# Two-block kernel: output and down projections as seven block products instead of eight

## The chip, the cores and the metric

The program runs on one core of a Trainium2 chip, in float32 throughout. The metric is the device time of one execution in microseconds (us), the median of several runs. Engines are named PE (matmuls), VectorE (DVE in rows), ScalarE (ACT), GpSimd (POOL) and SyncE (SP, which issues the weight loads).

## The reference, cut to what matters

The model has a first block (four mixers and a routed mixture of experts) and, behind it, two layers of a second kind of block, which are where the change lies. For 528 rows (16 meta rows and 4 tiles of 128 tokens) each layer computes, with `alpha = 4 ** 0.25`:

```python
m = concat(retention, pooling, attention)      # rows x 1024
h = layer_norm(alpha * h + m @ w_out)           # output projection, 1024 x 1024
u = silu(h @ w_ffn1) * (h @ w_ffn3)             # rows x 2816
h = layer_norm(alpha * h + u @ w_ffn2)          # down projection, 2816 x 1024
```

## The kernel before

Only the two layers matter here. Each layer `l` is worked in two runs, named by `x`: run A holds tiles 1 and 2 (and the meta rows, tile 0, in layer 0), run B tiles 3 and 4. `TILES`, `WHOLE` and `SPAN` say which rows that is. PE's program for the layers is `layers()`: `project` (input projection), `mix` (output projection), `turn_rows` (transposes of normalised rows, copied out by ScalarE), `feed_up` (gate and up projections, one pair for each of 22 blocks `f` of 128 features) and `feed_down`. The feed is done in two chunks, `FF_CHUNKS`: c = 0 has 12 blocks, c = 1 has 10. The order around the joints is: `mix(0,A)`, the last four feature items of `project(0,B)`; `feed(0,A)`, `mix(0,B)`, `project(1,A)`; `feed(0,B)`, `mix(1,A)`, `project(1,B)`; for (1,A) both chunks of `feed_up` and the first `feed_down`, then `mix(1,B)`, then `feed_down(1,A,1)`, then `turn_rows("mid",1,B)` and `feed(1,B)`.

**Projections as items.** An output projection of a run is four items (two tiles by two halves of 512 output columns), each a chain of 8 matmuls 128x512 over k into one PSUM bank (L1579). A down projection is four items of 12 or 10 matmuls (L1610). With run A in layer 0 comes an item for the 16 meta rows (L1570, L1613). One `pe.matmul` in float32 is two passes in the trace, so 8 matmuls are 16 rows there. VectorE adds each bank to the residual `h2` (L3129, L3191), and normalises a tile when its second half is there (`norm_rows`, L2746 to L2764; `norm_centered` and `norm_scaled` at the end of a feed). In both, ScalarE gives the root of the variance between two steps (`rows_root`, L1869); where in ScalarE's order this stands is written out by hand in its `layers()`, for example `roots(3)` ahead of `project(1,A)`, which begins with the copies of `turn_rows("start",1,A)`.

**Banks.** All items share the ring `main` of three banks. An item waits until the bank of the item three before it is drained.

**Weights.** Pieces of 2 MB go in program order through a ring of four slots (`LAYER_SLOTS`), loaded by SyncE (L1785). Piece n is loaded when piece n-4 is done with, which is marked by `piece_free[at] = main.done()`. `weights(l, n)` makes PE wait for the piece's landing. An output projection has two pieces, one for each half of the columns; a down chunk has three. Piece order at two joints, with the slots: the three of `feed_down(0,A,1)` in slots 2, 3 and 0, then the two of `mix(0,B)` in 1 and 2; the two of `mix(1,B)` in 2 and 3, then the three of `feed_down(1,A,1)` in 0, 1 and 2.

**Attention.** `attend(l, x)` is a generator of steps (`Plan`), run on every engine with the same numbering and taken one by one with `each(steps)` between items: before every block of `feed_up` and before every item of `feed_down`. Steps from `fox_at` on (17 in plan B, 14 in plan A) are softmax attention: PE writes scores (L1485), VectorE adds the bias and takes the maximum (L3061 to L3075), ScalarE exponentiates, VectorE scales (L3084), and the next step's transposes on PE wait for that (`fox_weights_ready`).

**GpSimd** only issues the loads of the norms' parameters in the layers (L1831), each behind the event that frees the buffer `ln_par2`.

## Time and profile before

| | |
|---|---|
| median of 3 runs | 3264.47 us (3263.72 to 3269.08) |
| span of the profiled execution | 3252.7 us |
| PE busy | 3120.2 us, 96% of the span |
| VectorE, ScalarE, GpSimd busy | 975.8, 540.8, 47.2 us |
| layers | about 1735 us to the end of the span |

The profiled execution is one of its own; the page gives its span, not its time between host and end. The span is 11.8 us under the median of the runs: start and end of the program lie around it. PE's busy time says how long at least one pass was in flight; the time of one pass is its group's busy time by its count.

### The profile page before, as it was taken

The numbers are of one execution on the slowest core, as the hardware profiler recorded it, in microseconds if no ns is written. First come the engines' busy times: TensorE is split into PE (matmuls) and PEld (weight loads), VectorE is DVE, ScalarE is ACT, GpSimd is POOL, SyncE is SP. The second block draws the span as 40 slices with busy tenths as digits, with TensorE's granted clock in tenths as the row PEclk, the third lists the DMA queues.
The fourth block names the chain that finished last, engine by engine and source line by source line (L and its number), as shares of the span: only waits on it lengthen the run. The fifth ranks groups of instructions, "written<-read, shape, count | busy, mean of one in ns | idle before, by whom it ended". The sixth has DMA issues, their size and how long they took to land.

```text
span 3252.7 us, 52666 instructions
## 1 busy us (share of the span) xinstructions
PE 3120.2 (96%) x22631; PEld 1747.5 (54%) x22631; DVE 975.8 (30%) x2146; ACT 540.8 (17%) x1129; POOL 47.2 (1%) x58
## 2 busy tenths in 40 slices
PE   9878989999999999999999999999999999999999
PEld 3355545333343333333345668574785758675866
DVE  1633455232223223222363431223023122132101
ACT  1332311111111111111122220130102100040000
POOL 0000002000000000000010000000000000000000
PEclk9888979999999999999989999999999999999999
DMA  9800115999999999999863333234333243243532
GB/s 400 354 1 27 53 53 224 386 410 403 408 397 406 400 406 407 407 407 404 351 251 119 125 130 117 111 143 176 135 126 142 105 194 133 100 176 116 195 145 100
DMA packets 97466, 743.70 MB, mean 229 GB/s; under 512 B 11128, under 2 KB 38336, under 8 KB 57552
## 3 DMA queue, kind: packets, MB, share of 16 engines
q1 hardware_dynamic: 58768, 687.49, 53.6%
q10 hardware_dynamic: 32624, 30.52, 2.9%
q0 software_dynamic: 5968, 24.14, 1.9%
q8 instruction: 83, 1.36, 0.2%
q14 instruction: 23, 0.19, 0.0%
HBM read 674.98 MB, written 67.13 MB: 228 GB/s over the span
## 4 chain that ended last, share of the span: by engine, by line
PE 55%; DMA 28%; DVE 3%; ACT 2%; issue 1%; ACTq 1%; POOL 0%; DVEq 0%
DMA arena<-x_sorted 27%; PE psum L1593 19%; PE psum L1610 9%; PE psum L1540 5%; PE psum L1579 3%; PE psum L1551 3%; PE psum L1244 1%; PE psum L802 1%; ACTq L587 1%; PE psum L1355 1%; PE psum L820 1%; PE psum L1196 1%; PE psum L1319 1%; PE psum L1411 1%; PE psum L1457 1%
## 5 line engine op out<-in xcount | busy, mean ns | idle before, releaser
L1244 PE MATMUL psum<-weight_ring,arena 128*32 128x512 f32 x6192 | 680.8, 594 | 23.6 <-DVE arena L2862 21.7
L1593 PE MATMUL psum<-arena,weight_ring 128*128 128x256 f32 (+1 forms) x2816 | 632.2, 383 | 3.1 <-ACT arena L2226 3.1
L1593 PEld LDWEIGHTS psum<-arena,weight_ring 128*128 128x128 f32 x2816 | 527.6, 189 | 99.0 <-issue 11.0
L1244 PEld LDWEIGHTS psum<-weight_ring,arena 128*32 128x32 f32 x6192 | 199.7, 110 | 485.5 <-issue 464.3
L1319 PE MATMUL psum<-weight_ring,arena 128*32 128x256 f32 x6144 | 338.2, 380 | 0.0
L1610 PE MATMUL psum<-weight_ring 128*128 128x512 f32 x704 | 305.4, 593 | 4.2 <-DVE weight_ring L3149 4.2
L1319 PEld LDWEIGHTS psum<-weight_ring,arena 128*32 128x32 f32 x6144 | 196.6, 110 | 153.0 <-issue 26.8
L1610 PEld LDWEIGHTS psum<-weight_ring 128*128 128x128 f32 x704 | 132.9, 190 | 169.3 <-issue 162.5
L2884 DVE STREAM_TRANSPOSE arena<-arena 128x384 f32<-128x384 f32 x32 | 18.6, 580 | 630.8 <-DMA arena<-x_sorted 630.8
L3149 DVE TENSOR_TENSOR weight_ring<-weight_ring,psum 128x256 f32<-128x256 f32 (+1 forms) x88 | 37.5, 426 | 486.1 <-PE psum L1593 480.3
L1540 PE MATMUL psum<-weight_ring,arena 128*128 128x512 f32 (+2 forms) x512 | 170.0, 489 | 3.1 <-ACT arena L2226 3.1
L818 PE MATMUL psum<-arena,weight_ring 128*128 128x512 f32 x288 | 134.2, 617 | 10.9 <-DMA weight_ring<-weights 6.6
L1540 PEld LDWEIGHTS psum<-weight_ring,arena 128*128 128x128 f32 x512 | 96.0, 190 | 70.5 <-issue 59.8
L2273 ACT ACTIVATE weight_ring<-psum 128x256 f32<-128x256 f32 (+1 forms) x88 | 34.1, 387 | 513.2 <-PE psum L1593 513.0
L1551 PE MATMUL psum<-arena,weight_ring 128*128 128x272 f32 (+1 forms) x512 | 117.1, 387 | 0.0
L2103 ACT ACT_TABLE_LOAD x32 | 41.1, 1283 | 428.0 <-issue 428.0
L1579 PE MATMUL psum<-weight_ring,arena 128*128 128x512 f32 x256 | 110.6, 592 | 0.0
L1551 PEld LDWEIGHTS psum<-arena,weight_ring 128*128 128x128 f32 x512 | 95.9, 189 | 19.1 <-issue 2.0
L818 PEld LDWEIGHTS psum<-arena,weight_ring 128*128 128x128 f32 x288 | 54.5, 196 | 76.8 <-issue 67.2
L3191 DVE SCALAR_TENSOR_TENSOR arena<-arena,psum 128x512 f32<-128x512 f32 x32 | 22.1, 690 | 232.5 <-PE psum L1610 232.5
L820 PE MATMUL psum<-weight_ring,arena 128*128 128x512 f32 (+1 forms) x192 | 90.8, 601 | 0.0
L2109 ACT COPY arena<-psum 128x256 f32<-128x256 f32 x96 | 36.0, 375 | 293.2 <-PE psum L1319 280.0
(435 smaller groups left out, 2532.0 us busy)
## 6 DMA issues: line engine op xcount, KB each, us to landing
weight_ring<-exp_gu SPq DMA_DIRECT2D x129, 2048.0 KB, 11.9
weight_ring<-weights SPq DMA_DIRECT2D x104, 2048.0 KB, 7.8
weight_ring<-exp_down SPq DMA_DIRECT2D x64, 2048.0 KB, 11.5
x_sorted<-arena SPq DMA_DIRECT2D x2, 10752.0 KB
arena<-x_sorted ACTq DMA_DIRECT2D x132, 96.0 KB, 21.6
y_sorted<-arena ACTq DMA_DIRECT2D x128, 96.0 KB, 17.6
y_sorted<-arena SPq DMA_DIRECT2D x2, 5632.0 KB, 39.7
y_sorted<-arena SPq DMA_DIRECT2D x2, 5120.0 KB, 37.3
```

Of the source, the lines that this page charges most:

```text
L818: mm = pe.matmul(bank, w[:, k, a:a + P], x_t[:, k, :], start=(k == 0), stop=(k == KT - 1))
L820: mm = pe.matmul(bank[:, 0:width], x_t[:, k, t * P:(t + 1) * P], w[:, k, a:a + width], start=(k == 0), stop=(k == KT - 1))
L1244: mm = pe.matmul(psum[j * GROUP:(j + 1) * GROUP, g, :], xg[:, k // 4, g, k % 4 * GROUP:(k % 4 + 1) * GROUP], w[:, kk, j * 512:(j + 1) * 51 ...
L1319: mm = pe.matmul(psum[j * GROUP:(j + 1) * GROUP, 3 + g, 0:256], hid_t[:, g, k * GROUP:(k + 1) * GROUP], w[:, kk, j * 256:(j + 1) * 256], s ...
L1540: mm = pe.matmul(bank[:, 0:width], h2_t[:, k, OFF[t]:OFF[t] + P], w[:, k, 0:width], start=first, stop=last)
L1551: mm = pe.matmul(bank[:, 0:b - a], w[:, k, c:c + P], h2_t[:, k, a:b], start=first, stop=last)
L1579: mm = pe.matmul(bank, h2_t[:, k, OFF[t]:OFF[t] + P], ws[half][0][:, k, :], start=(k == 0), stop=(k == KT - 1))
L1593: mm = pe.matmul(bank[:, 0:b - a], w[:, k, col:col + P], h2_t[:, k, a:b], start=(k == 0), stop=(k == KT - 1))
L1610: mm = pe.matmul(bank, ff_t[:, f, OFF[t] - a:OFF[t] - a + P], w[:, half * 512:(half + 1) * 512], start=first, stop=last)
L2103: T.did(act.activation(sig[:, g, :], swi[:, g, 0:256], ACT.Sigmoid, scale=SWIGLU_ALPHA), swish_given)
L2109: T.did(act.copy(y_out[:, g, :], psum[:, 3 + g, 0:256]), y_drained)
L3149: V.did(dve.tensor_tensor(g, g, bank[:, 0:b - a], ALU.mult), main.drained["v"])
```

## The change

Output and down projections of a run (all but the very last down chunk, layer 1, run B, c = 1) are computed as a 2 by 2 block product with seven block products in place of eight. The left blocks are (tile, parity of the k block), the right blocks (parity of the k block, half of the columns). `PRODUCTS` lists, in order, p1, p2, p7, p6, p3, p4, p5; each is a chain of 4, 6 or 5 matmuls 128x512 in one bank. Sums of left blocks are made by VectorE in place (four for each projection, and one in the new buffer `left_sum`); sums of weight blocks by GpSimd in place in the slots (four rounds for each, every round one instruction for a pair of pairs: two for an output projection, three for a down chunk). p6, p4 and p5 add to a bank that p1, p7 and p6 filled. The two weight pieces of an output projection are both asked for at its start and both marked free at its end. The meta item comes first, not last. Attention steps no longer stand in `feed_down` c = 0; a second step comes between gate and up of the blocks in `DOUBLE_STEPS`. Loads of norm parameters stand in GpSimd's queue between the rounds of sums. On VectorE the norms of a run's tiles follow after all seven products.

```diff
+DOUBLE_STEPS = dict(A=(4, 5, 6, 7, 8, 12), B=(5, 6, 7))
+DOWN_STEPS = (0, 2)
+PRODUCTS = (("p1", (0, 0), (0, 0), None, None), ("p2", (0, 1), (1, 0), None, None), ("p7", (1, 0), (0, 1), 1, 0),
+            ("p6", None, (0, 0), 2, 1), ("p3", (0, 1), (1, 1), 3, None), ("p4", (1, 1), (1, 0), None, 2), ("p5", (0, 0), (0, 0), 4, 3))
+ADDED_TO = ("p6", "p4", "p5")
...
-                ws = []
-                for half, t in rows_items(l, x):
-                    if t == WHOLE[x][0]:
-                        ws.append(weights(l, W_OUT + half))
...
-                    piece_free[ws[half][1]] = main.done()
+                ws, ats = zip(*(weights(l, W_OUT + half) for half in range(2)))
...
+                products(("mixed", l, x), KT // 2, pair_view(h2_t, 0, KT // 2, x), mix_blocks(ws), ready={"p2": fox_outs})
+                for at in ats:
+                    piece_free[at] = main.done()
+
+            def products(key, pairs, left, right, ready={}, steps=None, pace=()):
...
+                    bank = main.bank(pe)
...
+                    if left_sums is not None:
+                        pe.wait_ge(left_ready, 4 * (at - 1) + left_sums)
+                    for q in range(pairs):
+                        part, n = divmod(q, 2)
+                        if n == 0 and right_sums is not None:
+                            pe.wait_ge(right_ready, parts + right_sums * len(right) + part + 1)
...
+                        mm = pe.matmul(bank, stationary, right[part][f][half][:, n, :], start=(q == 0 and name not in ADDED_TO),
+                                       stop=(q == pairs - 1), skip_group_check=True)
...
                     for kind, by, col in (("gate", "a", 0), ("up", "v", 256)):
+                        if kind == "up" and f in DOUBLE_STEPS[x]:
+                            each(steps)
...
+            def product_sums(key, ats, right):
+                for at in ats:
+                    landed_piece(pool, at)
+                sums(right, (0, 1), (1, 1), ALU.subtract, (0, 1))
+                main.take(pool, (*key, "p1"))
+                G.settle()
+                sums(right, (0, 0), (0, 1), ALU.add, (0, 0))
+                main.take(pool, (*key, "p2"))
+                G.settle()
+                sums(right, (1, 0), (1, 0), ALU.subtract, (0, 0))
+                main.take(pool, (*key, "p6"))
+                G.settle()
+                sums(right, (0, 0), (1, 1), ALU.subtract, (0, 0))
...
+            load_norm(0, "ln_mid", (sem("layer_start"), NT2 + 3))
+            mix(0, "B")
...
+            def products(key, pairs, left, x, scale, stats):
...
+                def gather(name, t, part, by, out_of=None):
+                    bank = main.take(dve, (*key, name))
+                    row = h2[:, t, part]
+                    V.did(dve.scalar_tensor_tensor(row, row, by, bank, ALU.mult, ALU.add), out_of)
+
+                V.did(dve.tensor_tensor(a21, a11, a21, ALU.subtract), left_ready)
+                V.settle_other(left_ready)
+                V.did(dve.tensor_tensor(s2, a22, a21, ALU.subtract), left_ready)
+                gather("p1", t1, lo, scale, main.drained["v"])
...
+                gather("p5", t1, hi, 1.0)
+                gather("p5", t2, hi, 1.0, main.drained["v"])
+                V.settle_other(main.drained["v"])
...
+                products(("mixed", l, x), KT // 2, pair_view(h2_t, 0, KT // 2, x), x, ALPHA2, True)
+                dve.wait_ge(sem("layer_ln_landed"), 16 * landed)
+                for t in rows_of(l, x):
+                    norm_rows(V, h2[0:SIZE[t], t, :], t, ln_par2, sem("mid_ready"), SIZE[t], first_half=(t == 0))
...
+                    if c == 1:
+                        dve.wait_ge(sem("layer_ln_landed"), 16 * landed)
+                        for t in rows_of(l, x):
+                            norm_scaled(norm_centered(t), sem("layer_start"), parts)
```

**PE, start of the output projection of layer 0, run B**, before (each row one matmul instruction or several alike; landed_1 and landed_2 are the landings of slots 1 and 2):

```order
L1579 MATMUL psum<-weight_ring,arena 128x512 [waits fox_outs_drained,layer_weights_landed_1,main_drained_act,main_drained_dve,fox_turns_drained_dve,fox_turns_drained_act]
L1579 MATMUL psum<-weight_ring,arena 128x512 x6
L1579 MATMUL psum<-weight_ring,arena 128x512 [waits fox_outs_drained]
L1579 MATMUL psum<-weight_ring,arena 128x512 [waits main_drained_dve]
L1579 MATMUL psum<-weight_ring,arena 128x512 x7
L1579 MATMUL psum<-weight_ring,arena 128x512 [waits main_drained_dve,layer_weights_landed_2]
```

The same place in the changed kernel, p1 to the start of p6:

```order
L1632 MATMUL psum<-weight_ring,arena 128x512 [waits layer_weights_landed_1,fox_outs_drained,layer_weights_landed_2,main_drained_act,main_drained_dve,fox_turns_drained_dve,fox_turns_drained_act]
L1632 MATMUL psum<-weight_ring,arena 128x512 x3
L1632 MATMUL psum<-weight_ring,arena 128x512 [waits main_drained_dve]
L1632 MATMUL psum<-weight_ring,arena 128x512 x2
L1632 MATMUL psum<-weight_ring,arena 128x512 [waits fox_outs_drained]
L1632 MATMUL psum<-weight_ring,arena 128x512 [waits right_sums_ready,left_sums_ready,main_drained_dve]
L1632 MATMUL psum<-weight_ring,arena 128x512
```

The wait for slot 2 stood 16 matmuls into the projection and now stands at its first matmul.

**GpSimd, end of feed (0,A) and output projection (0,B)**, changed kernel (before, the first row alone stood here as a load of its own):

```order
L1896 DMA arena<-ln_mid 128x2048 [waits layer_start]
L1900 TENSOR_TENSOR weight_ring<-weight_ring 128x2x512 [waits layer_weights_landed_2,layer_weights_landed_1]
L1900 TENSOR_TENSOR weight_ring<-weight_ring 128x2x512
L1900 TENSOR_TENSOR weight_ring<-weight_ring 128x2x512 [waits right_sums_ready,main_filled]
L1900 TENSOR_TENSOR weight_ring<-weight_ring 128x2x512
```

The first round of sums is now behind the load that waits for the last norm of the feed before.

**PE, block f = 12 of feed (0,A)**, changed kernel (L1522 scores of an attention step, L1648 gate, then up; L839 transposes of the weights of the step before):

```order
L1522 MATMUL psum<-arena 128x400
L1648 MATMUL psum<-arena,weight_ring 128x272 [waits main_drained_dve,layer_weights_landed_1]
L1648 MATMUL psum<-arena,weight_ring 128x272 x7
L839 MATMUL psum<-arena,weight_ring 16x128 [waits fox_turns_drained_dve,fox_weights_ready]
L839 MATMUL psum<-arena,weight_ring 128x128 x3
```

Between scores and the wait for their softmax there stood 16 matmuls of gate and up; here it is the 8 of gate.

## Rows read from the trace of the kernel before

**Rows 1.** The page, part 1: engine, busy us, share, instructions.
```profile
PE 3120.2 (96%) x22631; PEld 1747.5 (54%) x22631; DVE 975.8 (30%) x2146; ACT 540.8 (17%) x1129; POOL 47.2 (1%) x58
```
**Rows 2.** Window: length; busy (instructions) of PE, PEld, DVE, ACT, POOL; PEclk, DMA, GB/s.
```profile
1900.00:2500.00 600.00, 594.33 (x2942) 404.15 (x2941) 161.70 (x321) 88.94 (x204) 1.60 (x3) 1.00 0.35 131
```
**Rows 3.** Groups from 1900 on: instructions, busy us, mean ns.
```profile
L1610 PE MATMUL psum<-weight_ring 128*128 128x512 f32 x704 | 305.4, 593 | 4.2 <-DVE weight_ring L3149 4.2
L1579 PE MATMUL psum<-weight_ring,arena 128*128 128x512 f32 x256 | 110.6, 592 | 0.0
```
**Rows 4.** PE's timeline at the end of feed (0,A): start us, length us.
```profile
2236.26 4.51 PE L1613 MATMUL psum<-weight_ring 128*16 128x256 f32 x80
2240.70 27.73 PE L1579 MATMUL psum<-weight_ring,arena 128*128 128x512 f32 x64
```
**Rows 5.** Two weight loads issued from 2240.8 to 2241.2: time to landing.
```profile
DMA to landing us min/median/max: 8.4/11.4/14.5
```
**Rows 6.** The load issued at 2612.9, start of output projection (1,A).
```profile
DMA to landing us min/median/max: 7.8/7.8/7.8
```
**Rows 7.** Timeline inside output projection (1,B), which lasts from 2951.2 to 2978.8.
```profile
2965.14 0.33 SPq L1785 DMA_DIRECT2D weight_ring<-weights  x1
```
**Rows 8.** Windows of 1 us behind a stop of PE in the first block.
```profile
480.00:481.00 1.00, 1.00 (x2) 0.42 (x2) 0.00 (x0) 0.00 (x0) 0.00 (x0) 0.50 0.99 410
481.00:482.00 1.00, 1.00 (x3) 0.38 (x2) 0.00 (x0) 0.00 (x0) 0.00 (x0) 0.95 0.89 377
```
**Rows 9.** PE's timeline there, with the idle time ahead in brackets.
```profile
472.67 3.68 PE L802 MATMUL psum<-arena 128*128 128x128 f32 x16 [5.65 <-DVE arena L2479]
477.02 12.57 PE L1187 MATMUL psum<-weight_ring 128*128 128x512 f32 x24 [0.68 <-ACT weight_ring L1878]
```
**Rows 10.** Timeline of all engines at the end of output projection (0,B).
```profile
2268.27 2.70 PE L802 MATMUL psum<-arena 128*128 128x128 f32 x24
...
2268.47 0.69 DVE L3129 SCALAR_TENSOR_TENSOR arena<-arena,psum 128x512 f32<-128x512 f32 x1 [1.80 <-PE psum L1579]
2268.91 2.38 ACT L2226 COPY arena<-psum 128x512 f32<-128x512 f32 x5 [4.62 <-PE psum L802]
2269.30 1.29 DVE L2746 BATCH_NORM_STATS2 arena<-arena 128x6 f32<-128x512 f32 x2
2270.62 0.21 DVE L2757 BATCH_NORM_AGGREGATE arena<-arena 128x2 f32<-128x12 f32 x1
2270.86 1.29 DVE L2760 SCALAR_TENSOR_TENSOR arena<-arena 128x1024 f32<-128x1024 f32 x1
2271.17 0.30 ACT L1869 ACTIVATE arena<-arena 128x1 f32<-128x1 f32 x1
2271.34 1.98 PE L1540 MATMUL psum<-weight_ring,arena 128*128 128x512 f32 x4 [0.37 <-ACT arena L2226]
```
**Rows 11.** Timeline behind down chunk (1,A,1).
```profile
3013.01 2.18 PE L802 MATMUL psum<-arena 128*128 128x128 f32 x16
...
3016.30 1.99 PE L1593 MATMUL psum<-arena,weight_ring 128*128 128x256 f32 x8 [1.11 <-ACT arena L2226]
```
**Rows 12.** PE's timeline behind output projection (0,A): the four feature items.
```profile
1933.22 14.08 PE L1551 MATMUL psum<-arena,weight_ring 128*128 128x256 f32 x64
```
**Rows 13.** Timeline of two attention steps of run (0,B), at f = 12 and 13.
```profile
2105.76 0.99 DVE L3061 TENSOR_TENSOR weight_ring<-psum,weight_ring 128x800 f32<-128x800 f32 x1
...
2109.83 0.77 DVE L3084 TENSOR_SCALAR weight_ring<-weight_ring,arena 128x400 f32<-128x400 f32 x2
...
2119.24 0.90 DVE L3084 TENSOR_SCALAR weight_ring<-weight_ring,arena 128x528 f32<-128x528 f32 x2
```
**Rows 14.** PE's timeline at the second of these steps.
```profile
2113.11 1.13 PE L1485 MATMUL psum<-arena 64*128 64x512 f32 x4
...
2114.31 7.60 PE L1593 MATMUL psum<-arena,weight_ring 128*128 128x272 f32 x32
```
**Rows 15.** GpSimd's groups: its one elementwise group of one input.
```profile
L1799 POOL COPY arena<-arena 128x1024 f32<-128x1024 f32 x4 | 4.2, 1061 | 530.7 <-DVE arena L2764 530.7
```

202 lines of the change are left out of this document (150 added, 52 removed).

## Prediction

> **What bounds the kernel now.** First the page: PE is busy for 96% of the span, GpSimd for 47.2 us of it [rows 1]. Then the windows of the layers, where the change lies: PE 594.33 of 600 us at a granted clock of 1.00, that is the 2.4 GHz level [rows 2]. So there is nothing under PE: what PE no longer does is gained, and every wait of PE that the change opens is lost in full. Then the groups: a pass of 128x512 costs 305.4 / 704 = 0.434 us in the down projections and 110.6 / 256 = 0.432 us in the output projections (their "mean ns" is the latency, not the price) [rows 3]. The timelines show what stands at each joint; at the end of feed (0,A) PE goes on into the output projection with no gap [rows 4].
>
> **What is saved.** An output projection goes from 4 x 8 = 32 matmuls to 7 x 4 = 28, a down chunk from 48 to 42 (c = 0) or from 40 to 35 (c = 1). Four output projections save 16, the chunks 4 x 6 + 3 x 5 = 39. That is 55 matmuls, 110 passes: 32 x 0.432 + 78 x 0.434 = **47.7 us saved**. The meta items stay.
>
> **GpSimd's sums.** A sum is 128x1024 from two inputs; no row has such an instruction on GpSimd. The nearest is its copy of the same size with one input, 1.06 us [rows 15]. From below the price is that, 1.06; if the two inputs are read one after the other it is 2.1, which I take as the nearest; from above 3.0, which is 2.1 with GpSimd shut out for as long as VectorE is busy (161.7 of 600 us, 27%, [rows 2], rounded up). What can the products bear? One product of a down chunk c = 0 takes 12 passes, 5.2 us. Counted from the start of p1 the last product p5 starts at 31.2 and reaches its last pair of blocks at 34.7; GpSimd must have done 12 sums by then: 2.9 us for each. An output projection gives 22.5 us for 8 (2.8), a chunk c = 1 29.5 us for 10 (2.95). At 2.1 all are hidden under the products, **0 us**; at 1.06 too; at 3.0 the excess is 1.5 us in each of four output projections, 1.3 in four chunks c = 0 and 0.5 in three chunks c = 1: 13 us. The Trainium skill, GPSIMD Engine Reference, section 3.1, speaks against the change: it has a two-input `tensor_tensor` of 2048 float32 at 4497 ns on GpSimd, near twice VectorE's time, and calls VectorE the rule for elementwise work. Half of that, as an estimate, is 2.25 us; the sum would be the same by it, since it too is under the bearable price.
>
> **VectorE's sums** are four of 128x512 to 128x768; two-input passes of 128x1024 take 1.29 us there [rows 10], so at most 1.0 us each. With four more drains of 0.69 us [rows 10] a projection has about 7 us more VectorE work over some 24 to 36 us, on an engine that is 27% busy. The first sum is asked for by p7, two products in. Hidden, 0.
>
> **What waits newly.** I went through the joints; T is the end of a projection's last product.
>
> *Weights, three places.* The output projection now asks for both pieces at its first matmul. At (0,B) and (1,A) the second piece goes into the slot of the first piece of the down chunk just ended, so its load cannot start before T. It is issued then in the kernel before as well, and lands 8.4 us later [rows 5], 7.8 us at (1,A) [rows 6]; there it was hidden under 32 passes. With 0.2 us to the issue PE waits 8.6 and 8.0 us. The third place is `feed_down(1,A,1)`: its third piece takes the slot of the first output piece of (1,B), which used to be free after two items (the load at 2965.1, 13.7 us ahead of the end [rows 7]) and now is at T: 0.2 + about 7.9 = 8.1 us. Together **24.7 us lost**. Queued behind the waiting matmul is all of PE; GpSimd's sums need the same landings. What is late next at (0,B) is GpSimd: its first round stands behind the load of `ln_mid`, which waits for the third norm of the feed, about 13.5 us after T. Sums at T + 16 and T + 18, against p7 at about T + 17: roughly in step, and I put **1 us** for it and 1 us for the first use of the sums.
>
> *The clock after these gaps.* After 5.65 us without a matmul PE goes on at 472.67 [rows 9] at a granted clock of 0.50, the 1.2 GHz level, and is back only in the window from 481, though dense matmuls ran from 477.02 [rows 8, 9]. Between 4 and 8.3 us at half speed cost 2 to 4.2 us; the gaps here are longer and dense matmuls follow at once, so 2.3 each, **7 us lost**.
>
> *Transposes behind three projections.* ScalarE must take the root for the run's first tile ahead of the copies that PE's transposes need. The tile is now normalised only after T: two drains of 0.69, half the statistics 0.65, aggregate 0.21, root 0.30 [rows 10], with gaps T + 3.0. Then four or five copies at about 0.55 (x5 in 2.38, and fetches) [rows 10] bring PE on at T + 5.8 and T + 5.4, where it took 3.1 us at (0,B) (2268.27 to 2271.34) [rows 10] and about 2.8 at (1,A): 2.7 and 2.6 lost. Behind (1,A,1) there is a second root between the copies, which waits for the whole norm of tile 1 (two passes of 1.29 more) and the aggregate of tile 2: root at about T + 6.9, two copies, PE on at T + 8.2, against 3.3 us before (3013.01 to 3016.30) [rows 11]: 4.9 lost. **10.2 us**.
>
> *Feature items behind (0,A).* The four items take 14.08 us [rows 12], 3.5 each, and VectorE drains them, after the norms of three tiles: 1.6 us of drains, then 3.7 + 3.7 + 4.3 us by the same prices [rows 10]. The first drain ends at T + 13.9; the fourth item needs that bank and would start at T + 10.6. **3.4 us lost**.
>
> *Doubled steps.* At f = 12 of run A the steps 17 and 18 have only gate between them, and 18 and 19 only up, 3.8 us each (half of 7.60, [rows 14]). From the add to the scaled weights takes 4.8 us (2105.76 to 2110.60) [rows 13], some 5.9 from the first score; the wide unit takes 7.0 (2113.11 to 2120.14) [rows 13, 14]. PE has 4.7 and 5.0 us of work. So 1.2 + 2.0, a little more in layer 1 where gate is shorter: **7 us** for both layers. The other doubled steps are retention steps with one short pass on VectorE: 0.
>
> **Sum.** -47.7 + 24.7 + 2 + 7 + 10.2 + 3.4 + 7 = +6.6 us on a span of 3252.7; start and end of the program are untouched, so the median goes from 3264.5 to about **3271**. A measurement of this kernel can tell about 0.2%, 6.5 us, from no change: this is at that edge, on the slow side.
>
> **Rivals.**
>
> *GpSimd becomes the bound.* At 3.0 us a sum 13 us come on top: 3284; each further 0.1 us costs 11 us over the 110 sums. For it: GpSimd's copy has one input only, and the Trainium skill, SBUF — State Buffer, section Who interferes with whom, has GpSimd and a VectorE instruction with two SBUF inputs exclude each other for a whole instruction. As a mechanism here: four sums of VectorE in each projection block 4 us of GpSimd's time, which 12 x 2.1 = 25 us still bear within 34.7. It decides above 2.8 us a sum. Against it: VectorE is busy for 27% of the time only. At 3.0 to 3.2 us: 3284 to 3306.
>
> *The weight gaps do not open* (the faster side). If the second pieces are there at T, 24.7 + 7 us fall away; behind them come out the first left sum, which waits for the norms (6.8 us at (0,B), 2.6 at (1,A)), and GpSimd's late round (some 5 us): 3271 - 31.7 + 14.4 = 3254. It decides where the gaps, with their clock, come to less than some 8 us. Against it: the load at 2240.8 is issued at T in the trace as it is, and lands 8.4 us later.
>
> *Less than said, no difference.* The three clock losses are small because half speed lasts 4 us or is not entered, and the softmax steps catch up: 3271 - 9 = 3262. The rows of the other gaps speak for a loss of some size.
>
> **Chances.** Forecast (3265 to 3280) 0.5; GpSimd 0.2; gaps not open 0.14; less than said 0.16. Faster by over 0.2% (under 3258): the gap rival, 0.15. Within 0.2%: the last rival and half of the forecast's lower side, 0.38. Slower (over 3271): 0.47. The range reaches from the gap rival to GpSimd's 3.0 and a little: 3254 to 3292; the forecast's own is 3265 to 3280.
>
> **What would show it.** Passes at L1632: 770 rows for 880 at 0.43 us. PE's waits for DMA at three first matmuls, 8 us each, and half clock behind them; waits for ScalarE's copies of 5 and 8 us ahead of the input projections; one wait for VectorE at the fourth feature item; waits for the softmax at f = 12. Sums on GpSimd near 2.1 us and no wait of PE for them but at (0,B). Wrong it would be if such a sum took over 2.8 us, if the second piece was there at T, or if some step of attention, now ahead of its data, held PE elsewhere.

## The result and the profile after

| | before | changed |
|---|---|---|
| median | 3265.53 us (8 runs) | 3274.84 us (8 runs) |
| ratio | | 1.0034, 95% interval 1.0021 to 1.0048 |
| span of the profiled execution | 3252.7 us | 3268.1 us |

The change makes the kernel slower by 0.34%, some 11 us (the interval reaches from 7 to 16); the prediction was 3271 against 3264.5, +6.6.

The spans differ by 15.4 us, which is no measure of the change. In the runs of the changed kernel the time is 1.8 us above the span, so most of the 11.8 us between span and median before are not start and end of the program: the execution profiled there was some 10 us shorter than the median run.

The page of the changed kernel, busy time of the engines, beside [rows 1]:

```profile
PE 3075.5 (94%) x22521; PEld 1726.0 (53%) x22521; DVE 1088.2 (33%) x2234; ACT 544.8 (17%) x1133; POOL 321.7 (10%) x174
```

PE is busy 45 us less, VectorE 112 us more and GpSimd 275 us more, and the span is longer. The groups of PE from 1900 on (line, names, shape, count; busy us, mean ns; idle time ahead and who ended it), beside [rows 3]. L1632 are the products, L1648 gate and up, L1577 and L1588 the input projection, L839 transposes:

```profile
L1648 PE MATMUL psum<-arena,weight_ring 128*128 128x256 f32 (+1 forms) x2816 | 636.3, 385 | 5.7 <-ACT arena L2339 5.7
L1632 PE MATMUL psum<-weight_ring 128*128 128x512 f32 x468 | 207.1, 601 | 12.7 <-DMA weight_ring<-weights 8.7 <-DVE weight_ring L3306 4.0
L1632 PE MATMUL psum<-weight_ring,arena 128*128 128x512 f32 x302 | 137.3, 612 | 17.1 <-DMA weight_ring<-weights 16.1 <-POOL weight_ring L1900 1.1
L1577 PE MATMUL psum<-weight_ring,arena 128*128 128x512 f32 (+2 forms) x256 | 87.0, 500 | 1.2 <-ACT arena L2339 1.2
L1588 PE MATMUL psum<-arena,weight_ring 128*128 128x256 f32 (+1 forms) x343 | 78.9, 390 | 3.1 <-DVE arena L3237 3.1
...
L839 PE MATMUL psum<-arena 128*128 128x128 f32 (+1 forms) x158 | 21.0, 271 | 5.2 <-ACT arena L2339 3.4 <-DVE arena L3255 1.8
L839 PE MATMUL psum<-arena,weight_ring 128*128 128x128 f32 (+2 forms) x144 | 20.4, 272 | 6.8 <-DVE weight_ring L3206 5.0 <-ACT weight_ring L2309 1.8
```

There are 770 passes at L1632, as counted; but they take 344.4 us, 0.447 each, where they would take 334 at 0.433. PE waits 24.8 us for weights (8.7 + 16.1). PE's timeline at the first of the three joints at which a projection follows on a projection, end of down chunk (0,A,1) to input projection (1,A) (start, length, count, in brackets the idle time ahead), beside [rows 4, 10]:

```profile
2246.11 12.92 PE L1632 MATMUL psum<-weight_ring,arena 128*128 128x512 f32 x24 [8.11 <-DMA weight_ring<-weights]
2259.38 1.96 PE L1632 MATMUL psum<-weight_ring,arena 128*128 128x512 f32 x4 [0.35 <-POOL weight_ring L1900]
2262.05 12.29 PE L1632 MATMUL psum<-weight_ring,arena 128*128 128x512 f32 x28 [0.71 <-POOL weight_ring L1900]
2274.17 1.04 PE L839 MATMUL psum<-arena 128*128 128x128 f32 x8
2275.80 0.63 PE L839 MATMUL psum<-arena 128*128 128x128 f32 x4 [0.60 <-DVE arena L3255]
2277.59 1.62 PE L839 MATMUL psum<-arena 128*128 128x128 f32 x12 [1.16 <-ACT arena L2339]
2279.58 12.83 PE L1577 MATMUL psum<-weight_ring,arena 128*128 128x512 f32 x23 [0.37 <-ACT arena L2339]
```

The wait for the second piece is 8.11 us, GpSimd's sums hold PE for 0.35 and 0.71 us, and the transposes take 5.4 us instead of 3.1. Windows of 2 us there (columns as in [rows 2]):

```profile
2246.00:2248.00 2.00, 1.89 (x3) 0.89 (x4) 1.97 (x3) 0.00 (x0) 0.00 (x0) 0.50 1.05 451
2248.00:2250.00 2.00, 2.00 (x4) 0.96 (x3) 1.90 (x5) 0.29 (x1) 0.00 (x0) 0.50 1.02 434
2250.00:2252.00 2.00, 2.00 (x5) 0.72 (x4) 1.93 (x3) 0.00 (x0) 0.76 (x2) 0.78 0.97 418
2278.00:2280.00 2.00, 1.63 (x12) 1.35 (x11) 1.93 (x4) 1.27 (x4) 0.00 (x0) 0.55 0.97 418
2280.00:2282.00 2.00, 2.00 (x3) 0.76 (x3) 1.90 (x5) 0.29 (x1) 0.00 (x0) 0.50 1.05 451
2282.00:2284.00 2.00, 2.00 (x3) 0.67 (x2) 1.13 (x1) 0.00 (x0) 0.54 (x1) 0.50 1.02 426
```

The granted clock is 0.50, the 1.2 GHz level, for some 4.8 us behind the gap, then again behind the transposes (short groups with 0.60, 1.16 and 0.37 us idle ahead of them): the input projection runs its first 5.4 us at that level (the window from 2284 to 2286 shows 0.74, the next 1.00). The trace of the kernel before has no such stretch from 1900 us until 3 us before its end.

From PE's timelines I made a table of stretches, each from its first matmul to that of the next, in us. It adds up to the time from the first output projection to the end of the span. (The block before it is the same code in both; the first output projection begins anywhere from 1894 to 1915 us in the traces of this study, so only this stretch is compared between traces.) There is one trace for each kernel, but stages that no edit touches agree closely in all thirteen traces with the change: 27.75 or 27.76 us for output projection (0,A), 111.38 to 111.48 for the rest. What differs from one execution to the next is where half speed occurs, and that moves the sum by some us, as shown below.

| stretch | before | changed | last experiment |
|---|---|---|---|
| output projection (0,A) | 31.18 | 27.76 | 27.75 |
| four feature items, transposes | 17.52 | 22.44 | 17.43 |
| feed (0,A) to the second down chunk | 250.99 | 248.37 | 245.83 |
| down chunk (0,A,1), output (0,B), transposes | 69.61 | 76.33 | 69.84 |
| input projection (1,A) | 81.37 | 84.07 | 81.37 |
| feed (0,B) to the second down chunk | 225.57 | 222.21 | 222.24 |
| down chunk (0,B,1), output (1,A), transposes | 64.74 | 70.06 | 63.79 |
| input projection (1,B) | 72.60 | 72.60 | 72.60 |
| feed (1,A) to output (1,B) | 235.59 | 233.40 | 234.01 |
| output (1,B), down chunk (1,A,1), transposes | 65.09 | 72.41 | 66.33 |
| feed (1,B) to the last chunk's blocks | 124.96 | 122.29 | 119.81 |
| rest | 111.44 | 111.48 | 111.41 |
| sum | 1350.7 | 1363.4 | 1332.4 |

Where no joint is in a stretch the products pay as counted: 3.4 us at the first output projection (4 matmuls). In feed (1,B), which is 2.67 us shorter in all, the down chunk alone gives 41.31 - 36.15 = 5.2 us (6 matmuls), and 2.5 are lost ahead of it. Each of the three joints, at (0,B), (1,A) and (1,A,1), gives back more than its two projections save.

### The profile page after: what moved, and what is told of

It reads as the page before. It is cut to its first block, busy times and chain, and to the rows that moved or that the text cites. A ratio compares the mean times of both kernels' runs of the same rounds, so it can differ in the third digit from the quotient of the medians.

```text
span 3268.1 us, 52768 instructions
## 1 busy us (share of the span) xinstructions
PE 3075.5 (94%) x22521; PEld 1726.0 (53%) x22521; DVE 1088.2 (33%) x2234; ACT 544.8 (17%) x1133; POOL 321.7 (10%) x174
## 4 chain that ended last, share of the span: by engine, by line
PE 53%; DMA 26%; DVE 4%; issue 2%; POOL 2%; ACT 2%; ACTq 1%; DVEq 0%; POOLq 0%
DMA arena<-x_sorted 25%; PE psum L1648 19%; PE psum L1632 9%; PE psum L1577 5%; PE psum L1588 3%; PE psum L1281 3%; PE psum L1356 2%; PE psum L839 1%; PE psum L1392 1%; ACTq L597 1%; PE psum L1233 1%; POOL weight_ring L1900 1%; PE psum L857 1%; PE psum L1679 1%; PE psum L1448 1%
## 5 line engine op out<-in xcount | busy, mean ns | idle before, releaser
L1648 PE MATMUL psum<-arena,weight_ring 128*128 128x256 f32 (+1 forms) x2816 | 636.3, 385 | 5.7 <-ACT arena L2339 5.7
L1648 PEld LDWEIGHTS psum<-arena,weight_ring 128*128 128x128 f32 x2816 | 529.1, 190 | 102.0 <-issue 11.9
L1900 POOL TENSOR_TENSOR weight_ring<-weight_ring 128x1024 f32<-128x1024 f32 (+1 forms) x116 | 271.6, 2366 | 1050.7 <-DMA weight_ring<-weights 611.8
L1632 PE MATMUL psum<-weight_ring 128*128 128x512 f32 x468 | 207.1, 601 | 12.7 <-DMA weight_ring<-weights 8.7
L1577 PE MATMUL psum<-weight_ring,arena 128*128 128x512 f32 (+2 forms) x512 | 174.1, 498 | 3.1 <-ACT arena L2339 3.1
L1632 PEld LDWEIGHTS psum<-weight_ring 128*128 128x128 f32 x468 | 89.7, 193 | 126.5 <-issue 120.1
L1632 PE MATMUL psum<-weight_ring,arena 128*128 128x512 f32 x302 | 137.3, 612 | 17.1 <-DMA weight_ring<-weights 16.1
L1577 PEld LDWEIGHTS psum<-weight_ring,arena 128*128 128x128 f32 x512 | 97.7, 193 | 73.0 <-issue 62.3
L3255 DVE SCALAR_TENSOR_TENSOR arena<-arena,psum 128x512 f32<-128x512 f32 x88 | 59.6, 688 | 197.8 <-PE psum L1632 197.7
L1878 POOL DMA_INDIRECT weight_ring<-y_sorted,arena x16 | 18.3, 1146 | 1082.4 <-ACTq L2228 1074.7
L1588 PE MATMUL psum<-arena,weight_ring 128*128 128x272 f32 (+1 forms) x512 | 119.0, 391 | 3.1 <-DVE arena L3237 3.1
L1588 PEld LDWEIGHTS psum<-arena,weight_ring 128*128 128x128 f32 x512 | 97.1, 191 | 23.3 <-DVE arena L3237 3.5
L1632 PEld LDWEIGHTS psum<-weight_ring,arena 128*128 128x128 f32 x302 | 59.0, 197 | 93.1 <-issue 89.2
```

The costliest lines, as they stand in the source:

```text
L1577: mm = pe.matmul(bank[:, 0:width], h2_t[:, k, OFF[t]:OFF[t] + P], w[:, k, 0:width], start=first, stop=last)
L1588: mm = pe.matmul(bank[:, 0:b - a], w[:, k, c:c + P], h2_t[:, k, a:b], start=first, stop=last)
L1632: mm = pe.matmul(bank, stationary, right[part][f][half][:, n, :], start=(q == 0 and name not in ADDED_TO), stop=(q == pairs - 1), skip_gro ...
L1648: mm = pe.matmul(bank[:, 0:b - a], w[:, k, col:col + P], h2_t[:, k, a:b], start=(k == 0), stop=(k == KT - 1))
L1900: G.did(pool.tensor_tensor(b[out[0]][out[1]], b[one[0]][one[1]], b[other[0]][other[1]], op))
L3255: V.did(dve.scalar_tensor_tensor(row, row, by, bank, ALU.mult, ALU.add), out_of)
```

## The experiments

All are edits of the changed kernel and are compared with the kernel before; the changed kernel's own ratio is 1.0034. A ratio's interval is 0.0010 to 0.0021 to either side, 3 to 7 us, so smaller effects are read from the trace: "the stretch" is the sum of the table (1363.4 us in the changed kernel).

**The three gaps filled.** 9 useless matmuls 128x512 into a free bank, ahead of the wait:

```diff
-                ws, ats = zip(*(weights(l, W_OUT + half) for half in range(2)))
+                first = weights(l, W_OUT)
+                if (l, x) in ((0, "B"), (1, "A")):
+                    filler(9, first[0])
+                ws, ats = zip(first, weights(l, W_OUT + 1))
```

> The changed kernel with 9 matmuls 128x512 of no use (18 passes, 7.8 us at 0.433) put into each of the three waits for weights, ahead of output projections (0,B) and (1,A) and of down chunk (1,A,1); nothing else moves, and PE goes on when the weights land. Theory (half speed behind these gaps costs PE 2.0, 2.6 and 1.8 us, from 4.0, 5.3 and 3.6 us at granted clock 0.50): the layers' stretch gets 6 us shorter than the 1363.4 us of the changed kernel, the granted clock stays at 1.00 behind the three places, and the time goes from +11 to about +5 us over the kernel before. Rival (the clock falls for another reason than PE's idling, for instance the weight loads themselves): the clock is still 0.50 behind the three places and the stretch is the same or up to 1 us longer.

Ratio 1.0011 (0.9997 to 1.0024), stretch 1354.2. Groups of PE, L1640 the products, L1413 the filler:

```profile
L1640 PE MATMUL psum<-weight_ring 128*128 128x512 f32 x468 | 203.9, 594 | 4.9 <-DVE weight_ring L3317 4.3 <-DMA weight_ring<-weights 0.6
L1640 PE MATMUL psum<-weight_ring,arena 128*128 128x512 f32 x302 | 132.8, 594 | 3.3 <-POOL weight_ring L1911 3.3
...
L1413 PE MATMUL psum<-weight_ring 128*128 128x512 f32 x54 | 23.7, 592 | 0.0
```

PE's wait for weights has fallen from 24.8 to 0.6 us, the filler takes its place, and the products cost 336.7 us instead of 344.4, although the first of them comes at most 0.4 us sooner behind the projection before. So half speed followed from PE standing still, and not from the weight loads. Of the 7.7 us 1.5 belong to down chunk (0,B,0), where nothing was filled; 6.2 are the three gaps'. At (0,B) the gain was lost again: the stage is 75.97 us for 76.33, since the products now run into GpSimd's late sums (3.3 us of waits instead of 1.1). The three filled joints are 0.4, 2.9 and 2.1 us shorter, 5.4 in all; the other 3.9 of the 9.3 us come from half speed at places that the edit doesn't touch (see the next run).

**The small joints filled.** One such matmul ahead of each of the last groups of transposes, four behind those of (1,B), three ahead of the last feature item of (0,B):

```diff
+                joint = {("start", 1, "A"): (1, 1, 0), ("start", 1, "B"): (1, 1, 1), ("mid", 1, "B"): (1, 1, 4)}.get((key, l, x), (0, 0, 0))
...
+                filler(joint[2])
                 pe.wait_ge(*job)
```

> The changed kernel with matmuls 128x512 of no use in the small waits between layers: 1 ahead of each of the last two or three groups of transposes behind output projections (0,B), (1,A) and down chunk (1,A,1), 4 behind the latter's transposes, and 3 ahead of the last feature item behind (0,A). Theory (the clock term was short because half speed also follows these small joints: behind (0,B), behind (1,A,1) and behind the features about 2 to 3.5 us each of lost speed): clock 1.00 behind them, the stretch of the layers 6 to 9 us shorter than 1363.4, time about +3 us over the kernel before. Rival (the passes are slower for another reason, such as VectorE, GpSimd and PE on the same memory): the clock falls or not, but the passes behind stay as long and the stretch changes by less than 2 us.

Ratio 1.0014 (1.0002 to 1.0026), stretch 1356.2. Groups of PE, gate and up, and the rows of the input projection:

```profile
L1661 PE MATMUL psum<-arena,weight_ring 128*128 128x256 f32 (+1 forms) x2816 | 633.8, 384 | 2.2 <-ACT arena L2352 2.2
...
L1590 PE MATMUL psum<-weight_ring,arena 128*128 128x512 f32 (+2 forms) x267 | 86.8, 484 | 0.4 <-ACT arena L2352 0.4
```

Gate and up fall from 636.3 to 633.8 us and input projection (1,A) from 84.07 to 81.37 (by the table's stages; the rows of the input projection hold 267 passes here and 256 in the changed kernel). For the 2.5 us at gate and up, behind the transposes of (1,B), the theory holds: they are in all seven traces in which those transposes come late, and in none of the six in which the gap is filled or gone.

At four other places half speed comes and goes while the waits ahead stay the same, so that one trace can't tell there what an edit does:

- the features: 22.44 us, but 20.76 in the traces of the filled gaps, of no sums, of the late load and of the moved roots, each with the same wait of 3.07 us;
- input projection (1,A): 84.07 us, but 81.37 in those of the filled gaps and of the late load, with the same 0.60, 1.16 and 0.37 us among the transposes. What this run gains there need not be the filler's;
- down chunk (0,B,0): 39.23 us, but 37.76 in six of the twelve other traces;
- input projection (1,B): 72.60 us, but 74.1 to 74.3 in six other traces, with the same 0.60, 1.15 and 0.80 us among the transposes.

What decides it stays open. In the trace of the changed kernel these places hold 5.9 us of lost speed.

**No sums on GpSimd.** The kernel leaves out the sums of weight blocks and gives their semaphore counts at once; the products multiply blocks as they were loaded.

```diff
-                    G.did(pool.tensor_tensor(b[out[0]][out[1]], b[one[0]][one[1]], b[other[0]][other[1]], op))
+                    pool.sem_inc(right_ready, 1)
```

> The changed kernel without GpSimd's 116 sums of weight blocks (their semaphore counts are given at once, so the products multiply unsummed blocks and the output is another one). Theory (GpSimd's sums are hidden under the products; only 1.1 us of PE's waits at output projection (0,B) are theirs): 1 to 2 us less than the changed kernel, about +9.5 us over the kernel before. Rival (the sums slow VectorE, whose waits then hold PE at the joints, or slow PE's own reads of the weights): 5 us or more less, with VectorE's sums and drains shorter and the passes of the products under 0.447 us outside the half-speed windows.

Ratio 1.0017 (1.0005 to 1.0028), stretch 1356.9: 6.5 us less. The expectation and its rival both have a part. VectorE is busy 1039.5 us instead of 1088.2, with the same instructions. Its second left sum in the changed kernel, and here (rows of VectorE by shape), the changed kernel's:

```profile
L3259 DVE TENSOR_TENSOR arena<-arena 128x512 f32<-128x512 f32 x4 | 14.1, 3514 | 0.1
```

and of this run:

```profile
L3256 DVE TENSOR_TENSOR arena<-arena 128x512 f32<-128x512 f32 x4 | 2.8, 693 | 0.1
```

It takes 3.51 us against 0.69. In the changed kernel's timeline at (0,B), VectorE:

```profile
2250.97 0.69 DVE L3257 TENSOR_TENSOR arena<-arena 128x512 f32<-128x512 f32 x1
2251.69 5.33 DVE L3259 TENSOR_TENSOR arena<-arena 128x512 f32<-128x512 f32 x1
```

and GpSimd:

```profile
2251.80 20.05 POOL L1900 TENSOR_TENSOR weight_ring<-weight_ring 128x1024 f32<-128x1024 f32 x8
```

GpSimd's 8 sums take 2.5 us each, and VectorE's second one, of 0.69 us by itself, lasts 5.33 beside them, as long as two of GpSimd's. The same happens ahead of down chunk (0,B,0), where GpSimd takes up its sums (2453.70) as soon as the weights are there and VectorE still has the softmax of the last block; changed kernel:

```profile
2453.70 7.16 POOL L1900 TENSOR_TENSOR weight_ring<-weight_ring 128x1024 f32<-128x1024 f32 x3 [169.74 <-DMA weight_ring<-weights]
2454.03 2.07 DVE L3196 TENSOR_TENSOR weight_ring<-weight_ring,arena 16x32 f32<-16x32 f32 x1
...
2456.23 2.42 DVE L3196 TENSOR_TENSOR weight_ring<-weight_ring,arena 128x256 f32<-128x256 f32 x1
...
2462.94 3.46 PE L1632 MATMUL psum<-weight_ring 128*128 128x512 f32 x4 [2.50 <-DVE weight_ring L3306]
```

and without sums:

```profile
2453.65 0.18 DVE L3193 TENSOR_TENSOR weight_ring<-weight_ring,arena 16x32 f32<-16x32 f32 x1
...
2453.97 0.40 DVE L3193 TENSOR_TENSOR weight_ring<-weight_ring,arena 128x256 f32<-128x256 f32 x1
...
2460.57 3.70 PE L1632 MATMUL psum<-weight_ring 128*128 128x512 f32 x8 [0.52 <-DVE weight_ring L3303]
```

Two passes of 0.18 and 0.40 us take 2.07 and 2.42, and PE's wait for the last block of the feed goes from 0.52 to 2.50 us; it is 2.1 to 2.8 us in every trace that has the sums. Two things must be kept apart from this. The kernel before waits nearly as long at this place, behind other work of VectorE:

```profile
2450.89 3.70 PE L1610 MATMUL psum<-weight_ring 128*128 128x512 f32 x8 [2.18 <-DVE weight_ring L3149]
```

So against it 0.3 us are lost here; without GpSimd's sums the change would have gained 1.7. And the half speed behind the wait (39.23 against 37.77 us for the chunk) is not the sums': five traces that have them show 37.76.

Of the 6.5 us, then, 3.1 are waits of PE that follow from the sums (1.1 at (0,B), 2.0 here). Nearly all the rest is clock: 1.4 us at (0,B), where half speed lasts less long, and at the other places half speed that comes and goes, the 1.7 of the features among it.

**No doubled softmax step.** `A=(4, 5, 6, 7, 8, 12)` becomes `A=(3, 4, 5, 6, 7, 8)` in `DOUBLE_STEPS`.

> The changed kernel with the doubled attention step at f = 12 of run A moved to f = 3, so that softmax steps again stand one for each block. Theory (the doubled softmax steps hold PE by 5.0 us in the trace of the changed kernel, 1.5 + 0.8 in layer 0 and 1.7 + 1.0 in layer 1, where 7 were put): the waits of PE's transposes for the scaled weights fall from 5.0 to under 0.5 us and the time by 5 us, to about +6 us over the kernel before. Rival (all steps now come one block earlier, ahead of their data; retention steps at f = 3 hold PE instead): the waits move to f = 3 to 8 and the time stays within 2 us of the changed kernel.

Ratio 1.0013 (1.0000 to 1.0026), stretch 1356.8. PE's wait for the scaled weights, 5.0 us in L839's row above, has gone from the row, and nothing took its place; the attention work itself moved to earlier blocks:

```profile
L839 PE MATMUL psum<-arena,weight_ring 128*128 128x128 f32 (+2 forms) x150 | 21.2, 272 | 1.8 <-ACT weight_ring L2309 1.8
```

The two feeds of run A are 2.5 and 2.8 us shorter, 5.3 in all; the other 1.3 of the 6.6 us less in the stretch are clock elsewhere.

**Second pieces waited for late.**

```diff
+                        if late is not None and (name, q) == late[0:2]:
+                            landed_piece(pe, late[2])
```

> The changed kernel, but the second weight piece of output projections (0,B), (1,A), (1,B) is waited for only at p7, and the third piece of down chunk (1,A,1) only at the fifth matmul of p1; GpSimd still waits for all pieces. Theory (the three waits are for landings at 8.1 us behind the end of the projection before): at (1,A) p1 and p2, 6.9 us, lie in the wait and p7 then stands for GpSimd's first sum until about 10.6 us behind the end, 4 us gained; at (1,A,1) the wait shrinks from 8.7 to about 4.8, 3.5 to 4 us gained; at (0,B) nothing, because GpSimd's first sum and VectorE's first left sum come only at 16 us, as before. With less half speed about 9 us in all: +2 us over the kernel before. Rival (the products need GpSimd's and VectorE's sums so soon that the wait only moves to p7): under 3 us gained, waits of PE for GpSimd or VectorE of 6 us or more at each of the three places.

Ratio 1.0041 (1.0028 to 1.0055), stretch 1359.7. PE's timeline at (0,B):

```profile
2253.96 7.19 PE L1641 MATMUL psum<-weight_ring,arena 128*128 128x512 f32 x12 [9.44 <-POOL weight_ring L1910]
```

and at (1,A):

```profile
2627.82 20.03 PE L1641 MATMUL psum<-weight_ring,arena 128*128 128x512 f32 x40 [5.21 <-POOL weight_ring L1910]
```

The wait for the landing has become one for GpSimd's first sum, 9.4 us at (0,B), where nothing is gained, and 5.2 at (1,A), 2.9 us gained; at (1,A,1) 4.9 us of the wait for the piece are left, 2.8 gained. The trace has 3.8 us less in all, and the runs (five of them) show nothing of it: the rival was nearer.

**Late pieces, and the load of `ln_mid` behind the first round.** The run before, with this besides:

```diff
-            load_norm(0, "ln_mid", (sem("layer_start"), NT2 + 3))
-            mix(0, "B")
+            mix(0, "B", (0, "ln_mid", (sem("layer_start"), NT2 + 3)))
```

> As the run before (second pieces late), and in GpSimd's queue the loads of ln_mid ahead of output projections (0,B) and (1,A) stand behind the first round of sums instead of ahead. Theory A (at (0,B) GpSimd is late because of its queue): its sums start at the landing, 8.3 us behind the end of the feed, p7 waits for the first left sum only, some 2 to 3 us less than the run before. Theory B (a VectorE instruction with two inputs in SBUF stands still while GpSimd sums: in the changed kernel the second left sum took 5.3 us there where 0.69 is usual, and without GpSimd's sums all of them took 0.69): GpSimd's early sums then hold VectorE in the norm of the meta rows, whose passes of 1.27 us grow by 2 to 5 us, the left sums come later, and the time is the same as in the run before or up to 3 us more.

Ratio 1.0014 (1.0003 to 1.0024), stretch 1353.3. At (0,B) theory B is right. VectorE's timeline (norm of the meta rows, first left sum):

```profile
2254.85 1.70 DVE L3333 SCALAR_TENSOR_TENSOR arena<-arena 16x1024 f32<-16x1024 f32 x1
...
2256.66 3.17 DVE L3345 SCALAR_TENSOR_TENSOR arena<-arena 16x1024 f32<-16x1024 f32 x1
2259.87 0.69 DVE L3267 TENSOR_TENSOR arena<-arena 128x512 f32<-128x512 f32 x1
```

GpSimd's:

```profile
2252.48 6.28 POOL L1910 TENSOR_TENSOR weight_ring<-weight_ring 128x1024 f32<-128x1024 f32 x2 [11.86 <-DMA weight_ring<-weights]
```

and PE's:

```profile
2260.66 20.27 PE L1641 MATMUL psum<-weight_ring,arena 128*128 128x512 f32 x40 [9.23 <-DVE arena L3267]
```

VectorE's passes of 1.27 us take 1.70 and 3.17, and GpSimd's two sums take 6.28 us instead of 5: each stands while the other works. The stage at (0,B) takes 76.0 us as ever. At (1,A), where the load was in the way too, 0.9 us came out. Most of the 6.4 us between the two stretches is half speed missing at the features (1.7) and at input projection (1,A) (2.9), at places where it comes and goes.

**The root behind the copies.**

```diff
-                roots(3)
-                project(1, "A", mid_roots=(4,))
+                project(1, "A", mid_roots=(3, 4))
```

and likewise at (1,A) and (1,A,1).

> The changed kernel with ScalarE's root of the first tile put behind the copies of the transposes, at (0,B), (1,A) and (1,A,1), instead of ahead of them or between them. Theory (PE's transposes wait behind these three projections because ScalarE waits for the statistics first): PE comes on 3 us behind the end of a projection instead of 5.4, 5.4 and 7.6, that is 2.2 + 2.2 + 4.4 = 9 us, and up to 4 us more because the clock no longer falls there: about +1 us over the kernel before. Rival (a new wait takes its place, VectorE's norm gets its root later and the next drain on VectorE or the next projection's rows hold PE): under 4 us gained.

Ratio 1.0005 (0.9996 to 1.0015), stretch 1346.4, the most of any one edit. PE's timeline behind down chunk (1,A,1) in the changed kernel, beside [rows 11]:

```profile
3030.03 0.66 PE L839 MATMUL psum<-arena 128*128 128x128 f32 x4 [1.05 <-ACT arena L2339]
3034.33 10.94 PE L1648 MATMUL psum<-arena,weight_ring 128*128 128x256 f32 x38 [3.65 <-ACT arena L2339]
```

and in this one:

```profile
3021.01 1.07 PE L839 MATMUL psum<-arena 128*128 128x128 f32 x8 [0.60 <-DVE arena L3253]
3022.81 17.53 PE L1648 MATMUL psum<-arena,weight_ring 128*128 128x256 f32 x80 [0.73 <-ACT arena L2339]
```

The wait of 3.65 us falls to 0.73, and the 2.5 us of half speed behind it (86.14 to 83.66 us of gate and up) are gone. The three joints are 1.7, 2.3 and 4.2 us shorter, input projection (1,A) 2.7. The other 3.6 of the 17.0 us lie at the features and at feed (0,B), nearly all of it clock that comes and goes.

**Down chunk (1,A,1) plain** (`in_products` leaves it out as well).

> The changed kernel with down chunk (1,A,1) computed as before in four plain items of 10 matmuls instead of seven products of 5 (5 matmuls, 4.3 us more). Theory (the piece that lands late is asked for at the start of the chunk in either form, and the first output piece is freed late by (1,B) in either form, so the wait of 8.7 us and its 1.8 us of half speed stay; the transposes behind are early again, 4 us gained): within 2 us of the changed kernel. Rival (the wait belongs to the products): it goes, and the time falls by 6 us or more.

Ratio 1.0019 (1.0007 to 1.0030), stretch 1362.0; the plain items at L1679:

```profile
3002.53 36.53 PE L1679 MATMUL psum<-weight_ring 128*128 128x512 f32 x80 [8.37 <-DMA weight_ring<-weights]
```

8.37 us of wait stay, so the chunk's own form is not the cause of this gap; that it is the late freeing of the first output piece follows from the program and was not tried by itself. The stretch is within 2 us, as the theory had it; the two ratios allow anything from nothing to some 11 us less.

**First piece freed inside p5.**

```diff
+                        if frees is not None and (name, q) == ("p5", 1):
+                            mm.then_inc(sem("first_piece_free"), 1)
```

> The changed kernel, but the first weight piece of a down chunk is marked free at the second matmul of its last product p5 and not at its end, three matmuls (2.6 us) earlier in a chunk c = 1; the piece for the second half of output projections (0,B) and (1,A) takes that slot. Theory (the wait is the time from the end of p5 to the landing, 8.1 us): waits of 5.5 us at (0,B) and (1,A), 8.7 as before at (1,A,1), whose slot comes from an output projection; at (1,A) about 3 us gained, at (0,B) about nothing, because p7 there waits for GpSimd at 16 us behind the end in any case: 3 us less than the changed kernel. Rival (the landing is set by the queue, where the first piece of the projection is being loaded too): waits of 7 us or more and nothing gained.

Ratio 1.0023 (1.0004 to 1.0042), stretch 1363.0. PE's waits for weights ahead of the two output projections fall from 16.1 to 11.0 us, as expected, and at (1,A) 2.8 us came out; at (0,B) GpSimd took it (its waits rise from 1.1 to 3.6). Half speed behind other joints (1.7 us of it at input projection (1,B)) took the rest.

**All repairs together**, with the first two feature items drained between the norms.

> The changed kernel with all the single repairs together: late wait for second pieces and the loads of ln_mid behind the first round, the root behind the copies, no doubled softmax step, the first piece of a down chunk freed inside p5, and VectorE draining the first two feature items of (0,B) between the norms of (0,A). Theory (the losses are separate and add up): against the changed kernel -10 (e6), -13 (e7), -5 (e4), -3 (e9) and -3 us at the features in the layers' stretch of 1363.4 us, so some 1330 to 1335 us, 16 to 20 us under the kernel before, ratio 0.994 to 0.996. Rival (they hide one another, since GpSimd and VectorE are late next at each joint): half of it, a ratio of 0.998 to 1.000.

Ratio 0.9957 (0.9942 to 0.9971), stretch 1337.5: faster than the kernel before, and the stretch 2.5 us over the 1330 to 1335 of the theory. Of the 34 us that it added up 26 came out, where the rival had half.

**Left sums ahead of the norms.** The run before, with this besides (here the calls at (0,B)):

```diff
-                feed(0, "A", steps, 2)
-                each(steps, PLANS["B"].steps)
-                mix(0, "B", 3)
+                feed(0, "A", steps, 2, lambda: mix_left(0, "B"))
+                mix(0, "B", 3, True, lambda: norm_scaled(norm_centered(0), sem("layer_start"), 1))
```

> As the run before, and VectorE makes the first two left sums of output projections (0,B), (1,A) and of down chunk (1,A,1) ahead of the norms of the projection before instead of behind them; the meta rows' norm of (0,A) comes behind the drain of p2, GpSimd's load of ln_mid behind its third round. Theory (what is late next is the left sum behind the norms, 9.2 us of PE's waits at (0,B) and 4.7 at (1,A) in the kernel with late pieces): p7 waits for GpSimd's first sum only, about 10.6 us less 2.6 behind the end, 5 us less than the run before at (0,B) and 1 to 2 us at (1,A). Rival (VectorE's norms are slowed by GpSimd's sums and the drains of p1 behind them hold p6): the wait moves from p7 to p6 and at most 2 us are gained.

Ratio 0.9944 (0.9922 to 0.9965), stretch 1333.9. At (1,A) 2.7 us came out; at (0,B) nothing (75.29 and 75.18 us), as the rival had it: the wait has moved on, though to p3 and not to p6. PE's timeline there:

```profile
2247.34 12.23 PE L1641 MATMUL psum<-weight_ring,arena 128*128 128x512 f32 x24 [5.22 <-DVE arena L3294]
```

**The meta rows' norm behind p6.** In the run before, the call `between()` and GpSimd's load stand further back.

> As the kernel with the left sums first (ratio 0.9944), but at (0,B) the norm of the meta rows stands on VectorE behind the drain of p6 instead of ahead of the third left sum, and GpSimd loads ln_mid behind its last round. Theory (in that kernel PE waits 5.2 us for the third left sum at (0,B), because the meta rows' norm stands ahead of it and its two passes of 1.27 us take 2.69 and 3.17 beside GpSimd's sums): the wait goes from 5.2 to under 1 us, the stage from the start of down chunk (0,A,1) to the input projection from 75.2 to about 71 us. Rival (VectorE gets its turn only between GpSimd's sums, so the third left sum stays late behind the other work): 3 us or more of the wait stay, or the load of ln_mid, now late, holds the norms behind (0,B) and with them the transposes of (1,A).

Ratio 0.9930 (0.9915 to 0.9945), stretch 1332.4, the (0,B) joint 69.84 us instead of 75.18. (3.3 us at feed (0,B) and feed (1,A) came in again, 1.5 and 1.7 of it at their down chunks.) PE there:

```profile
2247.34 1.96 PE L1641 MATMUL psum<-weight_ring,arena 128*128 128x512 f32 x4 [1.82 <-POOL weight_ring L1914]
2250.54 1.98 PE L1641 MATMUL psum<-weight_ring,arena 128*128 128x512 f32 x4 [1.24 <-POOL weight_ring L1914]
...
2256.58 10.57 PE L1641 MATMUL psum<-weight_ring,arena 128*128 128x512 f32 x24 [0.71 <-POOL weight_ring L1914]
```

The wait for VectorE is gone; what stands there now is GpSimd, 0.7 to 1.8 us a time. This version is faster than both kernels: 0.7% under the one before (0.55 to 0.85%) and, by the two ratios, about 1% under the changed one. Against the run before the ratio shows no difference (the intervals overlap); the joint's 5.3 us are read from the trace.

## Why the prediction was right, and where its sum was short

The direction held, and so did the mechanism of most terms; the sum came out nearer than its terms, since some were too high and the clock was too low. Point by point:

- **Saved passes, -47.7.** 770 rows; an undisturbed projection is 3.4 and 5.2 us shorter. Right.
- **Weight waits, +24.7.** 24.8, three of them, the longest 8.7. Right, and so was the reason: freeing the slot 2.6 us earlier takes 5.1 us off the two of them whose slot that is.
- **GpSimd, +2.** PE waits 1.1 us for it. A sum takes 2.48 us for 128x1024 (row below), within the bearable 2.8, above the 2.1 taken and the estimate of 2.25. The rival that GpSimd becomes the bound did not come, but its mechanism, four sums of VectorE that block 4 us of GpSimd's time, looked at the lesser side: it is above all VectorE that stands.

```profile
L1900 POOL TENSOR_TENSOR weight_ring<-weight_ring 128x1024 f32<-128x1024 f32 x104 | 255.2, 2476 | 1050.7 <-DMA weight_ring<-weights 611.8 <-PE psum L1664 230.3 <-PE psum L1607 161.1
```

- **VectorE's sums, "at most 1.0 us each", hidden, 0.** Wrong in size, 3.5 us on average and up to 6.65 for the second one (5.33 for 0.69 at (0,B)), yet hidden: no wait of PE in the changed kernel is for them. What GpSimd's sums hold up on VectorE and PE does wait for is the softmax ahead of down chunk (0,B,0), 2.0 us against the run without sums and 0.3 against the kernel before. The Trainium skill, SBUF — State Buffer, section Who interferes with whom, says that a VectorE instruction with two SBUF inputs contends with a GpSimd instruction that reads SBUF, and that the ports which the two share are an exclusive lock; the traces agree, and show more than one instruction's length (5.33 us, two sums of 2.5).
- **Transposes, +10.2.** 8.7 by the timelines: 5.4 for 3.1, 4.9 for 2.8, 7.6 for 3.3. Moving the root took 8.2 us out of the three joints.
- **Features, +3.4** was 3.1; **doubled steps, +7** was 5.0.
- **The clock, +7.** This is the term that was mis-sized. For "the clock after these gaps" it is right: 4.8, 5.6 and 3.6 us at 0.50 behind the three gaps, by windows of the trace, would be 7.0 lost as an estimate, and filling them took 6.2 off the products. But the step counted no half speed behind any shorter joint. By the stages of the changed kernel's trace less those of traces without it there are 2.5 us at gate and up of (1,B), 2.7 at input projection (1,A), 1.7 at the features and 1.5 at down chunk (0,B,0): 8.4 us. In all 14.6, not 7. Only the 2.5 are there in every trace with the same waits; the other 5.9 come and go.
- Two small ones were not in the sum: PE's waits for the last block of features, 5.6 us instead of 4.2 [rows 3], and gate and up, 633.8 us where the same view of the kernel before has 632.2, both at full clock. What makes up the latter was not tried.

Summed anew: -47.7 + 24.8 + 1.1 + 8.7 + 3.1 + 5.0 + 14.6 + 1.4 + 1.6 = +12.6. The table has 12.8, the ratio 11 (7 to 16). That +6.6 lay as near as it did is in part luck: four terms were too high, by 4.7 us together (GpSimd 0.9, transposes 1.5, features 0.3, doubled steps 2.0), and hid part of the 10.6 us that the clock and the two small ones were too low.

The rival with no gaps was refuted by the trace. The rival with less loss had half speed brief or absent; the trace has it seven times. What GpSimd's sums cost in all is settled for the waits, 3.1 us against the run without them; what they cost through the clock is not, and the two ratios allow anything from nothing to some 11 us for the whole.

## What to carry to other kernels

Fewer passes on the bounding engine are worth their count only where nothing around them moves; here 48 us were saved and 60 given back, all but some 10 of it at four joints, by waits that each looked like a detail of order (both pieces asked for at once, a root ahead of the copies, norms ahead of a drain) and by the clock behind them. List what stands at each joint, price every gap twice, once as wait and once as clock, and repair in order; the waits behind come out one after the other, PE to GpSimd to VectorE. Don't take a difference of one or two us between two traces for the effect of an edit before the clock at that place is compared too. When elementwise work is put on GpSimd, look at VectorE's two-input instructions beside it, not only at GpSimd's own time.

## What the runs showed of the hardware that was not expected

- A VectorE instruction with two SBUF inputs stands through more than one of GpSimd's sums when these follow one another: 5.33 us for 0.69 beside sums of 2.5, and 6.65 for 0.82. Drains with one input in PSUM are not touched: 0.688 us on average with the sums, 0.689 without.
- PE's clock can fall behind joints in which it isn't idle for long: behind transposes with gaps of 0.60, 1.16 and 0.37 us input projection (1,A) lost 2.7 us, and behind a gap of 3.07 us the features lost 1.7. Neither is certain: with the same gaps the one was missing in two other traces and the other in four.
- Useless matmuls in gaps of 8 us keep the clock: with 54 passes more the products behind cost 6.2 us less and the three joints 5.4. The ratio is 1.0011 for 1.0034, with intervals that still overlap.
